# Another pitch for the hidden-state tiles of a two-layer decoder step: 272 and 288 words in place of 264

## The chip, the cores and the metric

One core of one Trainium2 chip runs the whole program in one launch. The metric is device time in microseconds (us), taken as the median of several runs. Engines are named as the profile names them: PE (TensorE matmul), PEld (TensorE weight load), DVE (VectorE), ACT (ScalarE), POOL (GpSimd) and SP (SyncE, which here only issues transfers).

## The reference

The program is one inference step of a two-layer decoder. It takes 264 tokens (256 of a prompt and 8 single-token samples), each a vector of 2048. Each layer is a mixer (retention, mLSTM and pooling heads behind one input projection and before one output projection) and a feed-forward block, which is the part that the change is about:

```python
def _layer(x, ...):
    ...                                        # mixers, x = x + rms_norm(mixed @ w_out)
    hn = _rms_norm(x, g_pre_ffn)
    ff = (jax.nn.silu(hn @ w_ffn_gate) * (hn @ w_ffn_up)) @ w_ffn_down
    x = x + _rms_norm(ff, g_post_ffn)
```

`w_ffn_gate` and `w_ffn_up` are 2048 x 5632, `w_ffn_down` is 5632 x 2048, all float32.

## The kernel before

**Products.** Activations lie transposed in the on-chip memory: 128 partitions hold 128 features, and a row of 264 words of 4 bytes holds the tokens. Each float32 product is made of three matmuls in a rounded float32 format (`F32R`): every weight and every activation is split into a high part and a low part, and high x high, high x low and low x high are added up in one PSUM bank. A matmul loads a weight tile of 128 x 128 (weight load, PEld) and streams an activation tile of 128 x 264 past it (PE). The function `chunk` (line 557) does this for a chunk of weights; its three parts follow each other, each over all tiles `k` of the chunk: `high` weights with the high tiles, `high` weights with the low tiles, `low` weights with the high tiles. Nearly all of these matmuls are recorded on line 572, and the few of a tile that is waited for last on lines 550 to 552.

**Stages of a layer.** The input projection and mixers run first, then the output projection (its activations are the tiles `mixed`), then the feed-forward block in two halves (`NBLK` = 2). Each half does gate and up projection for 22 hidden tiles (`BT` = 22; the activations are `ahi` and `alo`, 16 tiles each) and then the down projection (`down`, in PE's block): 16 output tiles, each from two chunks of 11 hidden tiles (`HT` = 11). So there are four down stages in the program. In a down stage the loop body is 8 chunks (four output tiles) and runs three times, with a last copy of it behind the loop.

**The hidden tiles.** For each hidden tile DVE multiplies the gate and up results, ACT copies the product into `hhi` (line 1245, which rounds it), and DVE subtracts to get the rest, `hlo` (line 1754). Line 634 hands both to the down projection as the streamed operand. `hhi` and `hlo` are laid over the region of `proj`, 48 tiles of 264 words, which the mixers have finished with by then.

**Where things lie.** `place` hands out regions of the on-chip memory one after the other, in bytes per partition: `x`, `ahi`, `alo` (16 x 264 words each), `raw` with `wlo` over it (4 x 2048 words), `whi` (2 x 2048 words), then `proj` with `mixed`, `hhi` and `hlo` over it. A tile `k` of `ahi`, `alo`, `hhi` or `hlo` starts `k` x 264 words behind the start of its array, so that consecutive tiles follow each other without a gap.

**Order of the work.** SP loads the weight chunks into four slots; ACT makes the high parts (line 941) and DVE the low parts (line 1306) two chunks ahead; DVE also empties the banks (lines 1711, 1741, 1745, 1771, 1773). All of it is tied together by counters written out by hand.

Of the kernel before, what the change touches and what calls it, by code (L numbers as in the profile page):

```python
# [18 lines left out]
F32R = mybir.dt.float32r  # L19
# [4 lines left out]
P = 128  # L24
D_MODEL, BATCH_S, SEQ, DEPTH, PAST = 2048, 8, 256, 2, 2048
TOK = SEQ + BATCH_S
# [8 lines left out]
BT = FT // NBLK  # L35
# [9 lines left out]
NPROJ = 48  # L45
# [97 lines left out]
FIRST_HI = [None, 0, 1, None]  # L143
AHEAD = [3, 4, 5, None]
SKEW = 4
UPDATES = [(0, 1), (1, 1)] + [(k, 2) for k in range(2, KT, 2)]
UPDATED_IN = [g for g, (_, n) in enumerate(UPDATES) for _ in range(n)]
N_UPD = len(UPDATES)
BANKS = 4
# [80 lines left out]
def build(nc, a, gamma, gchunk):  # L230
    with ExitStack() as ctx:
# [5 lines left out]
        def place(name, shape, dt, at=None):  # L237

            n = 4
            for s in shape[1:]:  # L240
                n *= s
            if at is None:
                at = used[0]
                used[0] += (n + 31) // 32 * 32
                assert used[0] <= 212800, (name, used[0])
            t = nc.alloc_sbuf_tensor_at(name, shape, dt, offset=start + at)
            return t, at
# [7 lines left out]
        x, _ = place("x", [P, KT, TOK], F32)  # L255
        ahi, _ = place("ahi", [P, KT, TOK], F32R)
        alo, _ = place("alo", [P, KT, TOK], F32R)
        raw, at_raw = place("raw", [P, RAW, CHUNK], F32)
        wlo, _ = place("wlo", [P, RAW, CHUNK], F32R, at_raw)
        whi, _ = place("whi", [P, HI, CHUNK], F32R)  # L260
        proj, at_proj = place("proj", [P, NPROJ, TOK], F32)
        mixed, _ = place("mixed", [P, NPROJ, TOK], F32R, at_proj)
        hhi, _ = place("hhi", [P, BT, TOK], F32R, at_proj)
        hlo, _ = place("hlo", [P, BT, TOK], F32R, at_proj + 4 * BT * TOK)
        table, _ = place("table", [P, sum(TABLE_SIZES)], F32)
        gains, _ = place("gains", [P, DEPTH, N_GAINS], F32)
        wpool, _ = place("wpool", [P, PG, P], F32)
        wgate, _ = place("wgate", [P, KT, 2 * MH], F32)
        gbias, _ = place("gbias", [P, DEPTH, 2], F32)
        sq, _ = place("sq", [P, 4, TOK], F32)  # L270
        ssq, _ = place("ssq", [P, TOK], F32)
        rms, _ = place("rms", [P, TOK], F32)
        rstd, _ = place("rstd", [P, TOK], F32)
        epsc, _ = place("epsc", [P, 1], F32)
        unread, _ = place("unread", [P, 1], F32)
        pick, _ = place("pick", [P, 4], F32)
        zero, _ = place("zero", [P, TOK], F32)
        ones_, _ = place("ones", [P, P], F32)
# [6 lines left out]
        def carve(region, at, *shapes):  # L285

            out = []
            for shape in shapes:
                n = 1
                for d in shape:  # L290
                    n *= d
                v = region[:, at:at + n]
                at += (n + 7) // 8 * 8
                if len(shape) == 2:
                    v = v.rearrange("p (a b) -> p a b", a=shape[0])
                if len(shape) == 3:
                    v = v.rearrange("p (a b c) -> p a b c", a=shape[0], b=shape[1])
                out.append(v)
            assert at <= region.shape[1] + 7, (at, region.shape)
            return out + [at]  # L300
# [7 lines left out]
        whi_spare, _ = place("whi_spare", [P, CHUNK], F32R, at_work + 4 * at_spare)  # L308
# [5 lines left out]
        selv, identv, maskv, rowsv, _ = carve(work, 0, (MH, P), (P,), (P,), (NR,))  # L314
# [9 lines left out]
        pa, pb, cut16, pwin, wsum, _ = carve(work, at_r, (PW,), (PW,), (16,), (PG, BATCH_S * 16), (PG, BATCH_S))  # L324
# [15 lines left out]
        gates, lfa, lfb, _ = carve(flat_sq, 0, (2, TOK), (TOK,), (TOK,))  # L340
# [3 lines left out]
        fourth_q, fourth_k, _ = carve(heads, 0, (KT, P), (KT, P))  # L344
        late = proj[:, T_MO:NPROJ, :].rearrange("p a t -> p (a t)")
        Cs, cdiag, _ = carve(late, 0, (BATCH_S, MV), (BATCH_S, MV))
# [155 lines left out]
        def _(pe):  # L502
            pe.wait_ge(*dve_done(3))
            for l in range(DEPTH):
# [75 lines left out]
                def first_three(c, o, m, e):  # L580

                    pe.wait_ge(*rms_made(l * 4 + e))
                    at_start = (l, m) == (0, 0)
                    skew = SKEW if at_start else 1
                    deferred = () if at_start else (2,) if m else (1, 2)
# [701 lines left out]
        def _(dve):  # L1287
# [6 lines left out]
            for l in range(DEPTH):  # L1294
# [27 lines left out]
                def scale_acc(m, k, n):  # L1322

                    u = 2 * l + m
                    dve.wait_ge(*acc_gained(u * KT + k + n))
                    dve.tensor_tensor(acc[:, k:k + n, :], acc[:, k:k + n, :],  # L1326
                                      rstd[:].rearrange("p (o t) -> p o t", o=1).broadcast_to([P, n, TOK]), ALU.mult)\
                        .then_inc(*scaled.up)

                def add_acc(g, k, n, done):  # L1330

                    dve.wait_ge(*scaled(g + 1))
                    dve.tensor_tensor(x[:, k:k + n, :], x[:, k:k + n, :], acc[:, k:k + n, :], ALU.add).then_inc(*done.up)  # L1333
# [11 lines left out]
                def into_operands(m, lay, m_next):  # L1345

                    c = lay * N_CHUNKS + (0, C_GU[0])[m_next]
                    base = (2 * l + m) * N_UPD
                    scale_acc(m, *UPDATES[0])
                    for g in range(N_UPD + 1):  # L1350
                        if g + 1 < N_UPD:
                            scale_acc(m, *UPDATES[g + 1])
                        if g < N_UPD:
                            add_acc(base + g, *UPDATES[g], x_updated)
                        if g >= 1:
                            k, n = UPDATES[g - 1]
                            for i in range(n):
# [695 lines left out]
```

## Time and profile before

| | us |
|---|---|
| median of 3 runs | 2467.01 |
| lowest and highest of them | 2466.32, 2468.39 |
| span of the profiled execution (first to last instruction) | 2466.6 |
| PE busy in that span | 2435.6 |

The time of the profiled execution itself is not listed apart from the three runs; its span is 0.4 us below their median. The page puts PE at 99% of the span and PE weight loads at 97%, DVE at 57%, ACT at 44%, POOL at 10%. A record of a matmul runs from its first streamed column to the end of its way through the array, so that the records of consecutive matmuls overlap: each lasts about 284 ns, and one starts every 121 ns.

### The profile page before, as it was taken

Reading aid. Unit: us, or ns where it says so; the run is one execution under the profiler, and the core shown is the slowest. Engines: PE = TensorE matmul, PEld = TensorE weight load, DVE = VectorE, ACT = ScalarE, POOL = GpSimd, SP = SyncE. Lnnn points to the kernel's source line nnn. Section 1 sums busy time; section 2 is a strip of 40 time slices with the busy share of each in tenths; the row PEclk is TensorE's granted clock in tenths of the full one; section 3 lists DMA queues with packets and bytes.
Section 4 is the critical chain, followed back from the end, with each engine's and each line's share of the span. In section 5 each row is a group of like instructions: output and inputs, shape, how many; then the busy total and the mean of one; then the engine's idle time right before and its main releaser. Section 6 shows DMA issues by size and latency. Waiting matters only on the chain.

```text
span 2466.6 us, 49136 instructions
## 1 busy us (share of the span) xinstructions
PE 2435.6 (99%) x20166; PEld 2387.1 (97%) x20166; DVE 1417.3 (57%) x1721; ACT 1088.0 (44%) x1419; POOL 246.2 (10%) x202
## 2 busy tenths in 40 slices
PE   9999999999999999999999999999999999999997
PEld 8999999899999999999999999998999999999997
DVE  5787564755544455554567866646555445555444
ACT  5444654543333343444444456545344333343443
POOL 1001334000000000002100014340000000000021
PEclk9999999999999999999999999999999999999999
DMA  8455545355545655545645555454555455555453
GB/s 301 164 172 197 196 164 187 137 180 177 187 159 185 202 174 184 183 159 184 222 151 169 173 200 197 167 175 139 185 182 177 167 183 195 187 175 182 163 185 130
DMA packets 71902, 443.87 MB, mean 180 GB/s; under 512 B 8656, under 2 KB 8880, under 8 KB 33136
## 3 DMA queue, kind: packets, MB, share of 16 engines
q1 hardware_dynamic: 64656, 415.40, 49.6%
q0 software_dynamic: 6992, 26.82, 3.5%
q8 instruction: 82, 1.34, 0.2%
q14 instruction: 28, 0.23, 0.0%
q10 hardware_dynamic: 144, 0.08, 0.0%
HBM read 427.10 MB, written 15.16 MB: 179 GB/s over the span
## 4 chain that ended last, share of the span: by engine, by line
PE 95%; DVE 3%; ACT 1%; issue 0%; DMA 0%; DVEq 0%; ACTq 0%
PE bank L572 86%; PE bank L550 1%; PE bank L551 1%; PE bank L552 1%; PE bank L651 1%; DVE work L1326 1%; PE bank L539 0%; DVE x L1333 0%; DVE wlo L1306 0%; PE bank L603 0%; PE bank L604 0%; PE bank L622 0%; PE bank L514 0%; DVE rstd L1319 0%; PE bank L816 0%
## 5 line engine op out<-in xcount | busy, mean ns | idle before, releaser
L1306 DVE TENSOR_TENSOR wlo<-raw,whi 128x2048 fp32r<-128x2048 f32 (+1 forms) x402 | 836.8, 2082 | 512.7 <-ACT whi L941 512.5
L941 ACT ACTIVATE whi<-raw 128x2048 fp32r<-128x2048 f32 (+1 forms) x406 | 709.4, 1747 | 883.8 <-PE bank L572 833.2
L572 PE MATMUL bank<-ahi,wlo 128*128 128x264 f32 x4096 | 537.9, 284 | 0.0
L572 PE MATMUL bank<-ahi,whi 128*128 128x264 f32 x4032 | 533.3, 285 | 0.0
L572 PE MATMUL bank<-alo,whi 128*128 128x264 f32 x4032 | 528.3, 284 | 0.0
L572 PEld LDWEIGHTS bank<-ahi,wlo 128*128 128x128 f32 x4096 | 512.2, 188 | 0.0
L572 PEld LDWEIGHTS bank<-ahi,whi 128*128 128x128 f32 x4032 | 505.0, 188 | 7.1 <-issue 3.1
L572 PEld LDWEIGHTS bank<-alo,whi 128*128 128x128 f32 x4032 | 503.9, 188 | 0.0
L572 PE MATMUL bank<-hhi,wlo 128*128 128x264 f32 x1392 | 190.1, 284 | 0.0
L572 PE MATMUL bank<-hlo,whi 128*128 128x264 f32 x1392 | 188.7, 283 | 0.0
L572 PE MATMUL bank<-hhi,whi 128*128 128x264 f32 x1392 | 188.6, 283 | 0.0
L572 PEld LDWEIGHTS bank<-hhi,wlo 128*128 128x128 f32 x1392 | 177.9, 188 | 0.1
L572 PEld LDWEIGHTS bank<-hhi,whi 128*128 128x128 f32 x1392 | 176.7, 188 | 0.0
L572 PEld LDWEIGHTS bank<-hlo,whi 128*128 128x128 f32 x1392 | 176.1, 188 | 0.0
L1818 POOL TENSOR_TENSOR ssq<-sq,ssq 128x264 f32<-128x264 f32 x56 | 118.5, 2117 | 264.2 <-ACT sq L963 264.2
L1245 ACT ACTIVATE hhi<-work 128x264 f32 (+1 forms) x88 | 37.4, 425 | 242.7 <-DVE work L1751 242.7
L1818 POOL TENSOR_TENSOR ssq<-sq,zero 128x264 f32<-128x264 f32 x4 | 8.6, 2160 | 1348.0 <-ACT sq L963 1329.9
L572 PE MATMUL bank<-mixed,whi 128*128 128x264 f32 x1016 | 128.4, 284 | 0.0
L572 PEld LDWEIGHTS bank<-mixed,whi 128*128 128x128 f32 x1016 | 125.4, 188 | 0.0
L1745 DVE TENSOR_TENSOR work<-bank,rstd 128x264 f32<-128x264 f32 x88 | 38.0, 432 | 135.1 <-PE bank L572 135.1
L1754 DVE TENSOR_TENSOR hlo<-work,hhi 128x264 f32 (+1 forms) x88 | 38.1, 433 | 60.1 <-ACT hhi L1245 60.1
L572 PE MATMUL bank<-mixed,wlo 128*128 128x264 f32 x508 | 68.0, 286 | 0.0
(311 smaller groups left out, 1817.2 us busy)
## 6 DMA issues: line engine op xcount, KB each, us to landing
raw<-w_gu SPq DMA_DIRECT2D x176, 1024.0 KB, 4.8
raw<-w_in SPq DMA_DIRECT2D x89, 1024.0 KB, 5.0
raw<-w_dn SPq DMA_DIRECT2D x128, 704.0 KB, 4.0
raw<-w_out SPq DMA_DIRECT2D x32, 1024.0 KB, 4.9
work<-s_ret POOLq DMA_DIRECT2D x12, 512.0 KB, 3.7
ret_s<-work POOLq DMA_DIRECT2D x12, 512.0 KB, 3.0
proj<-s_c POOLq DMA_DIRECT2D x8, 576.0 KB, 5.5
c_s<-proj POOLq DMA_DIRECT2D x8, 576.0 KB, 4.1
```

The lines of the kernel that those rows point to most:

```text
L550: pe.matmul(out, high[:, w], hi, start=first, stop=False)
L551: pe.matmul(out, high[:, w], lo, start=False, stop=False)
L552: return pe.matmul(out, low[:, w], hi, start=False, stop=last)
L572: mm = pe.matmul(out, weights[:, w], operand(tile)[of], start=start and part == 0 and k == 0, stop=stop and not late and part == 2 and k = ...
L651: return pe.matmul(out, in_, ident[0:n, 0:n], is_transpose=True, start=True, stop=True)
L941: act.activation(high[:, 0:words], raw[:, slot, 0:words], ACT.Copy).then_inc(*hi_made.up)
L1245: act.activation(hhi[:, i * 2 + u, :], hs[:, u, :], ACT.Copy).then_inc(*hidden_hi.up)
L1306: dve.tensor_tensor(wlo[:, slot, w], raw[:, slot, w], high[:, w].bitcast(F32), ALU.subtract)\
L1326: dve.tensor_tensor(acc[:, k:k + n, :], acc[:, k:k + n, :], rstd[:].rearrange("p (o t) -> p o t", o=1).broadcast_to([P, n, TOK]), ALU.mult)\
L1745: dve.tensor_tensor(ua[:, u, :], bank[j][:, 0:TOK], rstd[:], ALU.mult).then_inc(*tile_evac.up)
L1754: dve.tensor_tensor(hlo[:, i * 2 + u, :], hs[:, u, :], hhi[:, i * 2 + u, :].bitcast(F32), ALU.subtract).then_inc(*hidden_ready.up)
L1818: pool.tensor_tensor(ssq[:], sq[:, slot, :], zero[:] if first else ssq[:], ALU.add).then_inc(*sq_added.up)
```

## The change

The hidden tiles keep their size of 264 words, but the high tiles start every 272 words and the low tiles every 288 words, and the low array starts behind 22 x 272 words in place of 22 x 264. What lies between the tiles is left unused. Every instruction, its shape and its order stay as they are.

```diff
+PITCH_HI, PITCH_LO = 272, 288
...
-        hhi, _ = place("hhi", [P, BT, TOK], F32R, at_proj)
-        hlo, _ = place("hlo", [P, BT, TOK], F32R, at_proj + 4 * BT * TOK)
+        assert BT * (PITCH_HI + PITCH_LO) <= NPROJ * TOK
+        hhi = place("hhi", [P, BT, PITCH_HI], F32R, at_proj)[0][:, :, 0:TOK]
+        hlo = place("hlo", [P, BT, PITCH_LO], F32R, at_proj + 4 * BT * PITCH_HI)[0][:, :, 0:TOK]
```

## Rows read from the trace of the kernel before

**Rows 1.** The page, busy time, share of the span and count of each engine.

```profile
PE 2435.6 (99%) x20166; PEld 2387.1 (97%) x20166; DVE 1417.3 (57%) x1721; ACT 1088.0 (44%) x1419; POOL 246.2 (10%) x202
```

**Rows 2.** Windows: length, busy us (count) PE, PEld, DVE, ACT, POOL; PEclk, DMA share, GB/s.

```profile
451.00:714.00 263.00, 260.99 (x2147) 257.76 (x2148) 148.86 (x161) 109.98 (x127) 0.00 (x0) 0.99 0.49 168
714.00:841.50 127.50, 127.50 (x1059) 127.50 (x1058) 59.85 (x50) 45.19 (x33) 0.00 (x0) 1.00 0.56 187
...
2321.70:2449.30 127.60, 127.60 (x1057) 127.53 (x1056) 57.98 (x49) 55.42 (x64) 28.16 (x15) 1.00 0.49 164
...
455.00:456.30 1.30, 1.30 (x7) 1.11 (x6) 1.30 (x3) 0.80 (x4) 0.00 (x0) 0.50 0.00 0
```

**Rows 3.** Waits in the first down stage: total us, times, longest.

```profile
ACT whi L941 <- PE bank L572: 72.1, 27, 4.1
DVE wlo L1306 <- ACT whi L941: 52.0, 32, 2.9
```

**Rows 4.** The page's groups: one of three like it, and the writer of `hlo`.

```profile
L572 PE MATMUL bank<-hhi,wlo 128*128 128x264 f32 x1392 | 190.1, 284 | 0.0
...
L1754 DVE TENSOR_TENSOR hlo<-work,hhi 128x264 f32 (+1 forms) x88 | 38.1, 433 | 60.1 <-ACT hhi L1245 60.1
```

**Rows 5.** Timeline of PE, two like places in the first down stage: start, length.

```profile
753.48 0.28 PE L550 MATMUL bank<-hhi,whi 128*128 128x264 f32 x1
...
757.84 1.49 PE L572 MATMUL bank<-hhi,whi 128*128 128x264 f32 x11
...
817.23 0.28 PE L550 MATMUL bank<-hhi,whi 128*128 128x264 f32 x1
```

**Rows 6.** Timeline of PE in gate/up: parts of one chunk.

```profile
603.79 2.10 PE L572 MATMUL bank<-ahi,whi 128*128 128x264 f32 x16
605.73 2.10 PE L572 MATMUL bank<-alo,whi 128*128 128x264 f32 x16
```

**Rows 7.** Timeline of PE at 455 us, first and last of five.

```profile
455.11 0.42 PE L550 MATMUL bank<-ahi,whi 128*128 128x264 f32 x1
...
455.99 0.42 PE L604 MATMUL bank<-alo,whi 128*128 128x264 f32 x1
```

**Rows 8.** The tile `ahi`, eight instants: the two matmuls running, ns min/median/max.

```profile
L572 PE MATMUL bank<-ahi,whi x2: 282/284/285, 603.8 to 603.9; 128*128 128x264 f32 x2
L572 PE MATMUL bank<-ahi,whi x2: 282/283/284, 603.9 to 604.0; 128*128 128x264 f32 x2
L572 PE MATMUL bank<-ahi,whi x2: 282/283/284, 604.0 to 604.2; 128*128 128x264 f32 x2
L572 PE MATMUL bank<-ahi,whi x2: 278/280/282, 604.2 to 604.3; 128*128 128x264 f32 x2
L572 PE MATMUL bank<-ahi,whi x2: 278/280/283, 604.3 to 604.4; 128*128 128x264 f32 x2
L572 PE MATMUL bank<-ahi,whi x2: 283/286/288, 604.4 to 604.5; 128*128 128x264 f32 x2
L572 PE MATMUL bank<-ahi,whi x2: 288/288/288, 604.5 to 604.6; 128*128 128x264 f32 x2
L572 PE MATMUL bank<-ahi,whi x2: 285/286/288, 604.6 to 604.8; 128*128 128x264 f32 x2
```

**Rows 9.** The tiles `hhi` and `hlo`, instants at 758.0, 758.4 and 759.5 us.

```profile
L572 PE MATMUL bank<-hhi,whi x2: 278/280/282, 757.8 to 758.0; 128*128 128x264 f32 x2
...
L572 PE MATMUL bank<-hhi,whi x2: 288/288/288, 758.2 to 758.3; 128*128 128x264 f32 x2
...
L572 PE MATMUL bank<-hlo,whi x2: 279/280/282, 759.3 to 759.4; 128*128 128x264 f32 x2
```

**Rows 10.** Timeline of PE in the output projection: one chunk and the next start.

```profile
374.45 4.04 PE L572 MATMUL bank<-mixed,whi 128*128 128x264 f32 x32
378.33 2.12 PE L572 MATMUL bank<-mixed,wlo 128*128 128x264 f32 x16
380.29 0.90 PE L572 MATMUL bank<-mixed,whi 128*128 128x264 f32 x6
```

## The prediction

> **What bounds the kernel now.** I read the page first, for the engine that is busy: PE, with 2435.6 of 2466.6 us [rows 1]. Then windows over single stages, since a share over the whole program is a mean. In a down stage, the only stage whose reads the change moves, PE is busy for the whole window, 127.50 of 127.50 us, while DVE works 59.85 and ACT 45.19 [rows 2]; gate and up projection is as full, 260.99 of 263.00, the rest being its start. The waits of the first down stage run one way: ACT waits 72.1 us for PE to free a weight slot, DVE 52.0 us for ACT [rows 3], and PE is not in the list. So the reader is to see that here time is a count of matmuls times the distance from one start to the next, and nothing else; what the other engines do has some 65 us of room in each down stage.
>
> The count: four down stages, 32 chunks each, 33 matmuls a chunk, 4224, of which 1408 each are high weights on `hhi`, high weights on `hlo`, low weights on `hhi` (1392 of each stand on line 572 [rows 4], the other 16 on lines 550 to 552). The distance: the same matmul of the loop body comes at 753.48 and, two bodies of 264 matmuls on, at 817.23 us [rows 5], so 63.75/528 = 120.74 ns. 4224 of these are 510.0 us, the sum of the four windows. In gate and up projection 16 matmuls take 605.73 - 603.79 = 1.94 us, about 121 ns [rows 6].
>
> Is 120.7 ns a floor? No row shows one there. At 455 us the granted clock is 0.50, the 1.2 GHz level [rows 2], and five matmuls of the same size start 0.88/4 = 0.22 us apart [rows 7], which is just 264 columns at 1.2 GHz. In the down stages the clock is 1.00 [rows 2], the 2.4 GHz level; half of 220 ns is 110, and 10.7 ns are on top. So at the upper level something other than the array's clock slows the stream, and the question is whether the place of the streamed tile has a part in it.
>
> The Trainium skill (TensorE: Matmul & The Clock Gate, Back-to-back issue gap) gives N/2.4 + 2.5 ns for a matmul alone at the upper clock, 112.5 ns here; the trace disagrees, with 120.7. If the change brought the down stages to that figure, 8.2 ns x 4224 = 35 us would go, an estimate from that page.
>
> **Does the place matter? What the rows show.** A matmul's recorded length contains its time on the stream. At eight instants in a row of one gate/up chunk two matmuls are running, tiles 0 and 1, then 1 and 2, and so on [rows 8]. Pair by pair this solves to lengths of tiles 0 to 7: 285, 282, 284, 282, 278, 283, 288, 288 ns, and tile 8 is 285 again. The tiles are 1056 bytes apart, 4 x 256 + 32, so tile k starts at 32k modulo 256 bytes, and after eight tiles the place comes round. Is it the place, or the position in the chunk? In the down projection the 11 tiles from 757.84 us [rows 5] are tiles 11 to 21 of `hhi`: line 550 closes the second chunk of the body, the third takes 4 us, and this is the fourth, which like every second chunk takes the upper 11 tiles. `ahi` starts 16896 = 66 x 256 bytes into the arena, and `proj`, where `hhi` starts, at 99840 = 390 x 256, so both count from the same place. The first two, 11 and 12, last 278 and 282, the fourth and fifth, 14 and 15, both 288 [rows 9]: what tiles 4 and 3, 6 and 7 of `ahi` have. So the place goes with the length, over a range of 10 ns. But the law is not clean: `hlo` starts 22 x 1056 bytes further on, which is 192 modulo 256, so its tiles 12 and 13, the second and third of that chunk, stand where tiles 2 and 3 of `ahi` do, and last 279 and 282 in one order or the other, not 284 and 282 [rows 9]. What came before also counts, and a new order of places can settle on a new pattern.
>
> **The change, part by part.**
>
> *The places.* The high pitch is 1088 bytes, 4 x 256 + 64: the tiles start at 0, 64, 128, 192 modulo 256, with 6, 6, 5 and 5 of 22 tiles. Lengths by place: 6 x 285 + 6 x 284 + 5 x 278 + 5 x 288 = 6244, mean 283.8 ns. The low array starts 22 x 1088 = 23936 bytes on, 128 modulo 256, and its pitch of 1152 is 4 x 256 + 128, so low tiles start at 128 and 0 in turn: (278 + 285)/2 = 281.5 ns. Two in three matmuls stream `hhi`, one in three `hlo`: 283.05 ns. Before, all eight places: 2270/8 = 283.75. The difference is 0.70 ns a matmul, and 0.70 x 4224 = 3.0 us gained.
>
> Bounds of this term, from the same rows: every matmul at the best place, 278 against 283.75, -5.75 x 4224 = -24 us; every one at the worst, 288, +18 us. Between them I take the sum by places, because the two arrays go through four and two places and a mean over places has held elsewhere: 120.7 and 121 ns in two stages with different arrays.
>
> The Trainium skill (SBUF — State Buffer, Specifications (TRN2)) gives lines of 16 bytes and says that a read pays for each new line of 16 bytes that it crosses into. A tile is 66 such lines at all three pitches, so by that rule the term is 0 and the time stays. The lengths of 278 to 288 ns for equal tiles show that it is not the whole of it.
>
> *The gaps.* Consecutive tiles no longer touch (32 bytes of gap in `hhi`, 96 in `hlo`). The nearest rows are the output projection, whose tiles are taken out of order and partly apart: a chunk of 48 takes 380.29 - 374.45 = 5.84 us, 121.7 ns each, and its last 16, the low weights, 1.96 us, 122.5 ns [rows 10]. Against 120.74 that is +0.9 to +1.8 ns, on 4224 matmuls +4.0 to +7.5 us. That chunk differs in places as well as in gaps, so I count nothing of it in the sum and keep it as a rival.
>
> *The writers.* ACT and DVE write the 88 high and 88 low tiles at new places; the low ones take 433 ns each [rows 4]. If the place changed that by as much as a matmul's, 10 in 284, it would be 15 ns each, under 3 us for both kinds together, in a stretch where DVE idles 60.1 us just before these very instructions [rows 4]. Counted at nothing. If that cover were gone, only the last tile of each of four halves is waited for directly: 4 x 2 x 15 ns, 0.1 us.
>
> *What else might be late.* Nothing is added to a queue, no transfer or wait moves. If the down stages ran as fast as 110 ns a matmul, they would last 116 us, against 60 us of DVE and a DMA share of 0.56 [rows 2], so no other engine becomes the bound.
>
> *Sum.* 2466.6 us of span and the 0.4 us by which the median lies above it, less 3.0: 2464.0 us.
>
> **The rivals.**
>
> 1. *A worse order.* The new order of places and gaps settles like that of the output projection. Place: the down stages; price +0.9 to +1.8 ns a matmul, up to 2467.0 + 7.5; I name +1.4 ns, 2473. It decides for slower from +1.17 ns on (4.9 us). For it: those rows, and that the down stages are now at the lowest distance of the three stages shown. Against: the low tiles avoid the two places with 288 ns altogether.
>
> 2. *A good lock.* With only two places in turn for `hlo` and four for `hhi`, the stream settles at the quick end and stays there. The low tiles of [rows 9] ran at 279 and 282, mean 280.5, 3.25 ns below 283.75. Over all matmuls this is -13.7 us; over two thirds of them -9.2 us. I name 2456. For it: lengths depend on what came before, so a short cycle of places need not give the mean. Against: nothing picks the quick end over the slow one.
>
> 3. *The 10.7 ns go.* If they come from an awkward start of the tiles, and starts at multiples of 64 bytes cure it, 10.7 x 4224 = 45 us: 2422. Against it: before, every second tile already starts at a multiple of 64 relative to the array, and those four lengths (285, 284, 278, 288, mean 283.75) are no better than the other four (282, 282, 283, 288, also 283.75).
>
> 4. *The place is not the cause*, and the lengths follow a rhythm of PE itself that only looks like it: 2467.
>
> **How the numbers follow.** One measurement of this kernel can tell about 0.2%, 4.9 us, from no change. The sum by places 0.42, its own range 2460 to 2468 (1 ns a matmul either way, as far as the stages differ); a worse order 0.18; a good lock 0.30; the full gain 0.03; no effect 0.07. Faster by over 0.2%: 0.26 of the lock, 0.03, and 0.09 of the first case, 0.38. Slower: 0.16 of the worse order and 0.01 of the rest, 0.17. Within: 0.45. The range runs from the lock's full price of 13.7 us, 2453, to the worse order at 2474, and leaves out the far end of the lock, the full gain and +1.8 ns a matmul.
>
> **What would show it.** In the profile after: the distance of the same matmul over loop bodies (120.74 before) should be near 120.0; lengths of matmuls on `hlo` should take two values near 278 and 285, those on `hhi` four; gate and up projection must stay at 121. 119.5 or less shows the lock, 121.9 or more the worse order, 112 or so the full gain. The prediction is wrong if lengths do not follow places in the new order, so that the sum by places has no ground, or if a stage that the change does not touch moves.

## The result and the profile after

| us | before | after |
|---|---|---|
| median of 9 runs each | 2467.31 | 2472.49 |
| lowest and highest | 2466.27, 2468.39 | 2471.92, 2475.11 |
| span of the profiled execution | 2466.6 | 2473.3 |

The ratio is 1.0024, 95% interval 1.0014 to 1.0033. The change makes the kernel 5.2 us slower where 3.0 us less were forecast.

First the page after: its busy times, and the three groups of down-stage matmuls (count, busy us, mean ns of one record).

```profile
PE 2443.1 (99%) x20166; PEld 2395.0 (97%) x20166; DVE 1418.1 (57%) x1721; ACT 1088.3 (44%) x1419; POOL 247.9 (10%) x202
...
L576 PE MATMUL bank<-hhi,wlo 128*128 128x264 f32 x1392 | 192.7, 286 | 0.0
L576 PE MATMUL bank<-hlo,whi 128*128 128x264 f32 x1392 | 190.4, 284 | 0.0
L576 PE MATMUL bank<-hhi,whi 128*128 128x264 f32 x1392 | 189.1, 283 | 0.0
```

The last two of these groups before the change, beside the one of [rows 4]:

```profile
L572 PE MATMUL bank<-hlo,whi 128*128 128x264 f32 x1392 | 188.7, 283 | 0.0
L572 PE MATMUL bank<-hhi,whi 128*128 128x264 f32 x1392 | 188.6, 283 | 0.0
```

PE and its weight loads have grown, by 7.5 and 7.9 us; DVE and ACT stand within 1 us of where they stood [rows 1]. Of the three groups, low weights with `hhi` gained most, 190.1 to 192.7 us [rows 4], although only the places of activations were moved. Next the windows over the first down stage and the gate/up half behind it (columns as in [rows 2]).

```profile
715.40:844.20 128.80, 128.80 (x1058) 128.80 (x1057) 59.92 (x50) 45.17 (x33) 0.00 (x0) 1.00 0.56 186
844.20:1099.40 255.20, 255.20 (x2114) 255.20 (x2113) 135.87 (x131) 100.49 (x97) 0.00 (x0) 1.00 0.53 178
```

The stage took 127.50 us and now takes 128.80, with PE busy throughout and the granted clock at 1.00, the 2.4 GHz level, as before [rows 2]. So no wait has come in, and it is not the clock. The waits of that stage:

```profile
ACT whi L945 <- PE bank L576: 73.2, 27, 4.1
DVE wlo L1310 <- ACT whi L945: 52.4, 32, 2.9
```

They run the same way as in [rows 3] and have grown with the stage, by 1.1 and 0.4 us. Then PE's timeline: two parts in gate/up, the three parts of one chunk with the start of the next, and two like places two loop bodies apart (start, length).

```profile
605.23 2.10 PE L576 MATMUL bank<-ahi,whi 128*128 128x264 f32 x16
607.16 2.10 PE L576 MATMUL bank<-alo,whi 128*128 128x264 f32 x16
...
755.30 0.28 PE L554 MATMUL bank<-hhi,whi 128*128 128x264 f32 x1
...
755.67 1.49 PE L576 MATMUL bank<-hhi,whi 128*128 128x264 f32 x11
756.99 1.50 PE L576 MATMUL bank<-hlo,whi 128*128 128x264 f32 x11
758.33 1.52 PE L576 MATMUL bank<-hhi,wlo 128*128 128x264 f32 x11
759.69 0.53 PE L576 MATMUL bank<-hhi,whi 128*128 128x264 f32 x3
...
819.69 0.28 PE L554 MATMUL bank<-hhi,whi 128*128 128x264 f32 x1
```

The same matmul comes 64.39 us later, 64.39/528 = 121.95 ns a matmul, where [rows 5] give 120.74. In gate/up it is 1.93/16, about 121 ns, as in [rows 6]. The difference, 1.21 ns x 4224 = 5.1 us, is the whole of the medians' 5.2. The three parts of the chunk do not share it alike: 1.32, 1.34 and 1.36 us for 11 matmuls, 120.0, 121.8 and 123.6 ns.

Of the 6.7 us between the two profiled spans, 1.4 lie ahead of the first down stage, which starts at 715.4 in place of 714.0. Most of that is the clock's and not the change's. Windows over the first matmuls of gate/up, before and then after:

```profile
454.00:461.00 7.00, 6.40 (x42) 5.33 (x43) 7.00 (x15) 4.82 (x14) 0.00 (x0) 0.76 0.00 0
454.00:461.00 7.00, 6.36 (x32) 5.08 (x31) 7.00 (x14) 4.98 (x14) 0.00 (x0) 0.51 0.00 0
```

In these 7 us the mean granted clock was 0.76 in the execution before and 0.51 in the one after, which stood longer at the 1.2 GHz level (0.50). In other profiles it was 1.00 there (e6, e8) or 0.54 (e5), whatever the arrangement, so this is one part of the scatter of single times.

Last the tiles themselves: all matmuls on `hlo`, two pairs of neighbours among them, and the writers of both arrays, that of `hhi` after and before (ns minimum, median, maximum).

```profile
L576 PE MATMUL bank<-hlo,whi x1392: 281/283/289, 716.8 to 2454.5; 128*128 128x264 f32 x199
L576 PE MATMUL bank<-hlo,whi x2: 288/288/289, 761.1 to 761.3; 128*128 128x264 f32 x2
L576 PE MATMUL bank<-hlo,whi x2: 283/284/286, 761.5 to 761.6; 128*128 128x264 f32 x2
L1758 DVE TENSOR_TENSOR hlo<-work,hhi x88: 432/434/436, 484.2 to 2331.3; 128x264 f32 x76, 128x264 fp32r<-128x264 f32 x12
...
L1249 ACT ACTIVATE hhi<-work x88: 423/424/426, 483.7 to 2330.8; 128x264 f32 x76, 128x264 fp32r<-128x264 f32 x12
L1245 ACT ACTIVATE hhi<-work x88: 423/424/427, 482.3 to 2325.4; 128x264 f32 x76, 128x264 fp32r<-128x264 f32 x12
```

The low tiles start at two places only, 128 and 0 modulo 256 bytes, for which 278 and 285 ns were forecast. None lasts 278; two neighbours, one at either place, last 288 and 289, and a moment later a pair lasts 283 and 286. The writers have not changed: 424 ns for `hhi` as before, 434 for `hlo` after 433 [rows 4].

### The profile page after: what moved, and what is told of

The parts are those of the page before. It is cut to its first block, busy times and chain, and to the rows that moved or that the text cites. A ratio compares the mean times of both kernels' runs of the same rounds, so it can differ in the third digit from the quotient of the medians.

```text
span 2473.3 us, 49165 instructions
## 1 busy us (share of the span) xinstructions
PE 2443.1 (99%) x20166; PEld 2395.0 (97%) x20166; DVE 1418.1 (57%) x1721; ACT 1088.3 (44%) x1419; POOL 247.9 (10%) x202
## 3 DMA queue, kind: packets, MB, share of 16 engines
q8 instruction: 82, 1.34, 0.2%
## 4 chain that ended last, share of the span: by engine, by line
PE 95%; DVE 3%; ACT 1%; issue 0%; DMA 0%; DVEq 0%; ACTq 0%
PE bank L576 86%; PE bank L554 1%; PE bank L555 1%; PE bank L556 1%; PE bank L655 1%; DVE work L1330 0%; PE bank L543 0%; DVE wlo L1310 0%; DVE x L1337 0%; PE bank L607 0%; PE bank L608 0%; PE bank L626 0%; PE bank L518 0%; DVE rstd L1323 0%; PE bank L820 0%
## 5 line engine op out<-in xcount | busy, mean ns | idle before, releaser
L576 PE MATMUL bank<-hhi,wlo 128*128 128x264 f32 x1392 | 192.7, 286 | 0.0
```

The source lines that it names most:

```text
L576: mm = pe.matmul(out, weights[:, w], operand(tile)[of], start=start and part == 0 and k == 0, stop=stop and not late and part == 2 and k = ...
```

## Experiments

Below, "distance" is the time from the first to the last matmul of the first down stage, by their number less one; "parts" are its means over the chunks of the second and third loop body (without the chunk of lines 550 to 552), for high weights on `hhi`, high weights on `hlo`, low weights on `hhi`. Places are starts of the arrays, bytes modulo 256, `hhi` and `hlo`. A distance goes by the starts of matmuls alone, since the profile models their ends. It repeats within 0.01 ns where nothing in the down stages differs (e12 and e15, one kernel twice; before and e16, 120.73 both), far better than a device time does; 1 ns of it is 4.2 us.

| kernel | pitch in words; places | distance, ns | parts, ns | time, us | ratio [95%] |
|---|---|---|---|---|---|
| before | 264, 264; 0, 192 | 120.73 | 120.5, 120.6, 121.2 | 2467.5 | |
| after | 272, 288; 0, 128 | 121.96 | 120.8, 121.9, 123.3 | 2472.5 | 1.0024 [1.0014, 1.0033] |
| e1 | 272, 264; 0, 128 | 121.62 | 121.5, 120.7, 122.7 | 2471.0 | 1.0015 [1.0005, 1.0025] |
| e2 | 264, 288; 0, 128 | 121.84 | 121.6, 121.9, 122.0 | 2472.8 | 1.0023 [1.0013, 1.0032] |
| e3 | 264, 264; 128, 64 | 121.29 | 120.8, 122.4, 120.7 | 2470.1 | 1.0011 [1.0001, 1.0021] |
| e4 | 576, 576; 0, 128 | 121.42 | 121.0, 121.6, 121.5 | 2470.5 | 1.0013 [1.0003, 1.0022] |
| e5 | 264, 264, low read backwards; 0, 96 | 121.99 | 121.6, 121.8, 122.5 | 2474.7 | one run |
| e6 | 264, 312; 0, 96 | 121.99 | 121.6, 121.8, 122.5 | 2472.5 | one run |
| e7 | 272, 288; 128, 0 | 121.82 | 122.0, 122.1, 121.7 | 2472.7 | one run |
| e8 | 264, 264; 0, 96 | 120.98 | 120.6, 120.7, 121.4 | 2467.5 | one run |
| e9 | 264, 264; 0, 192, weights +128 | 121.29 | 120.8, 122.4, 120.7 | 2471.9 | one run |
| e10 | 576, 576; 0, 32 | 120.73 | 120.1, 121.1, 120.6 | 2467.5 | 1.0000 [0.9990, 1.0009] |
| e11 | 576, 576; 128, 160 | 120.78 | 120.0, 121.9, 119.9 | 2468.4 | one run |
| e12, e15 | 576, 576; 0, 224 | 120.29 | 119.8, 120.7, 120.1 | 2466.5 | 0.9996 [0.9987, 1.0005] |
| e17 | 272, 288; 0, 192 | 120.91 | 121.5, 119.9, 121.2 | 2469.2 | one run |
| e18 | 272, 288; 0, 160 | 121.69 | 121.0, 122.5, 121.2 | 2472.3 | one run |

The kernel before, run beside them, had medians of 2467.5 us (e1 to e4, e9 to e12) and 2467.3 (e13 to e16), and in one run each 2469.2 (e5 to e8) and 2468.2 (e17, e18). Where there was one run, the distance decides.

### Which part of the change costs? (e1 to e4)

**e1**, the high pitch alone, and **e2**, the low pitch alone, take the place of the two lines that lay out the tiles; so do the pairs of lines in the later diffs.

```diff
-        hhi, _ = place("hhi", [P, BT, TOK], F32R, at_proj)
-        hlo, _ = place("hlo", [P, BT, TOK], F32R, at_proj + 4 * BT * TOK)
# e1
+        hhi = place("hhi", [P, BT, 272], F32R, at_proj + 0)[0][:, :, 0:TOK]
+        hlo = place("hlo", [P, BT, 264], F32R, at_proj + 23936)[0][:, :, 0:TOK]
# e2
+        hhi = place("hhi", [P, BT, 264], F32R, at_proj + 0)[0][:, :, 0:TOK]
+        hlo = place("hlo", [P, BT, 288], F32R, at_proj + 23424)[0][:, :, 0:TOK]
```

> High tiles every 272 words, low tiles still every 264 (low array starts 128 bytes modulo 256 from the arena's base in place of 192). Mean distance of two matmuls in a down stage: 120.73 ns before, 121.96 after the change; by parts of a chunk (high weights on hhi, high on hlo, low on hhi) 120.5, 120.6, 121.2 before and 120.8, 121.9, 123.3 after. Theory A, the order of start places (modulo 256 bytes) sets the distance, with history over some tiles: the cost came mostly with the low tiles' two places, so about 121.0 here, parts 120.8, 120.6, 121.5, and about 2468.5 us. Theory B, every gap between consecutive tiles costs: two matmuls in three have a gap, 121.5 ns, parts 1 and 3 slow, part 2 not, about 2470.5 us. Theory C, the weights and the tile together (low weights on hhi are slow because of the pitch of hhi): parts 1 and 3 as after, 120.8 and 123.3, mean 121.5.

> Low tiles every 288 words at the same two places as after the change (128 and 0 modulo 256), high tiles still every 264. Theory A (order of places with history): part 2 as after, 121.9, part 3 partly, 122, part 1 as before, mean about 121.5, 2470.5 us. Theory B (gaps cost): only part 2 has gaps, 121.9, parts 1 and 3 as before, mean 121.1, 2468.8 us. Theory C (weights and tile together): part 3 as before, 121.2, mean 121.1.

Each costs most of the loss by itself, +0.89 and +1.11 ns, and both together +1.23, so the costs don't add. By itself e1 looks like Theory B, gaps: parts 1 and 3 are slow and part 2 is not. e2 speaks against it: the first part on `hhi`, whose tiles had neither moved nor got gaps, went from 120.5 to 121.6, and the mean to 121.84 where Theory B had 121.1. No part has a price of its own.

**e3**, the old pitches with both arrays 128 bytes further on, and **e4**, every tile at one of two places.

```diff
# e3
+        hhi = place("hhi", [P, BT, 264], F32R, at_proj + 128)[0][:, :, 0:TOK]
+        hlo = place("hlo", [P, BT, 264], F32R, at_proj + 23360)[0][:, :, 0:TOK]
# e4
+        pairs = place("pairs", [P, BT, 576], F32R, at_proj + 0)[0]
+        hhi, hlo = pairs[:, :, 0:TOK], pairs[:, :, 288:288 + TOK]
```

> Pitch 264 for both as before, but both arrays start 128 bytes further on. Theory A: lengths follow the place, so every length moves by four tiles along hhi (the shortest, 278 ns, stood at tile 12, now at tiles 8 and 16), while the mean distance stays, 120.7 ns and 2467 us. Theory D, a rhythm of PE that has nothing to do with the place: lengths stay at the tiles where they were, mean 120.7. Theory B expects no change of the mean either.

> High and low tiles in turn in one array with a pitch of 576 words, 2304 bytes = 9 x 256: every high tile starts at place 0 modulo 256, every low tile at place 128. Theory A: no variety of places, so the stream settles on one short pattern; its mean can lie anywhere in the range of lengths seen, 278 to 288 ns against a mean of 283.75, so a distance between 115 and 125 ns, clearly off 120.7 or 122.0, with few lengths. Theory B (gaps cost): every matmul has a gap, 122.5 ns or more, 2474 us or more. Theory D (place has no part): 120.7 ns, 2467 us, and eight lengths as before.

e3 was expected to leave the mean where it was, since its tiles go through all eight places as before; it came to 121.29. With all of `hhi` at place 0, e4 stands at 121.42, and its lengths are no one number: in long stretches they run through 288, 285, 278, 283, 283 and again, at one and the same place. In others they stand still. The first part of one and the same chunk of the loop body, without its first matmul, in the first body and in the second:

```profile
L572 PE MATMUL bank<-pairs,whi x10: 281/281/281, 732.7 to 733.8; 128*128 128x264 f32 x10
L572 PE MATMUL bank<-pairs,whi x10: 278/283/288, 764.7 to 765.8; 128*128 128x264 f32 x10
```

These are the same instructions, with the same tiles, weight slots and bank. They stand 120.0 ns apart in the first body and 121.7 in the second, in all four down stages alike, so what was streamed before them decides.

### Gaps, or places? (e5 to e8)

**e5** reads the low tiles backwards from an array without gaps; **e6** has the same places in the same order, 96 - 32k, with gaps of 192 bytes.

```diff
# e5
-                    return hhi[:, k, :], hlo[:, k, :]
+                    return hhi[:, k, :], hlo[:, BT - 1 - k, :]
...
-                                dve.tensor_tensor(hlo[:, i * 2 + u, :], hs[:, u, :], ...
+                                dve.tensor_tensor(hlo[:, i * (-2) + (BT - 1 - u), :], hs[:, u, :], ...
# e6
+        hhi = place("hhi", [P, BT, 264], F32R, at_proj + 0)[0][:, :, 0:TOK]
+        hlo = place("hlo", [P, BT, 312], F32R, at_proj + 23392)[0][:, :, 0:TOK]
```

> Pitch 264 for both, but the low tiles are stored in reverse, tile 0 last: they touch each other, and start places go back by 32 bytes modulo 256 from tile to tile, from place 96. This run stands beside e6_gap_back, which has the same start places modulo 256 with gaps. Theory A, only the sequence of start places modulo 256 and what went before count: both runs have the same lengths, matmul by matmul, and one mean distance, somewhere between 120.3 and 122.3 ns. Theory B, gaps cost: no gap here, so 120.7 ns here and over 121.1 in the other.

> High tiles every 264 words, low tiles every 312 words (1248 bytes, 224 modulo 256, so places go back by 32), low array starting so that tile k has the same place modulo 256 as in e5_low_reversed, with gaps of 192 bytes. Theory A: the same lengths and the same mean as there, within 0.1 ns. Theory B: part 2 of the chunks (high weights on hlo) slower by 1 ns or more than there.

The tile `hlo` of e5 and two like places of its timeline:

```profile
L572 PE MATMUL bank<-hlo,whi x1392: 281/284/288, 716.4 to 2454.1; 128*128 128x264 f32 x199
...
754.97 0.28 PE L550 MATMUL bank<-hhi,whi 128*128 128x264 f32 x1
...
819.38 0.28 PE L550 MATMUL bank<-hhi,whi 128*128 128x264 f32 x1
```

The same of e6:

```profile
L572 PE MATMUL bank<-hlo,whi x1392: 281/284/288, 714.3 to 2451.8; 128*128 128x264 f32 x199
...
752.83 0.28 PE L550 MATMUL bank<-hhi,whi 128*128 128x264 f32 x1
...
817.24 0.28 PE L550 MATMUL bank<-hhi,whi 128*128 128x264 f32 x1
```

Both take 64.41 us for two bodies, and matmul by matmul all 4224 lengths agree within 1 ns. Pitch and gap do not count; the places in their order do. And the order counts much: e5 reads the very places of before (all eight, in an array without gaps), and is 1.26 ns slower.

**e7** shifts the changed kernel's arrays by 128 bytes; **e8** keeps the pitches of before with the low array at e6's first place.

```diff
# e7
+        hhi = place("hhi", [P, BT, 272], F32R, at_proj + 128)[0][:, :, 0:TOK]
+        hlo = place("hlo", [P, BT, 288], F32R, at_proj + 24064)[0][:, :, 0:TOK]
# e8
+        hhi = place("hhi", [P, BT, 264], F32R, at_proj + 0)[0][:, :, 0:TOK]
+        hlo = place("hlo", [P, BT, 264], F32R, at_proj + 23392)[0][:, :, 0:TOK]
```

> The change's own pitches, 272 and 288, both arrays 128 bytes further on. If the loss belongs to the two pitches (or to their gaps), the mean distance stays at 122.0 ns. If it belongs to the sequence of places at which each part begins and the history that it carries over (Theory A as it stands after e3_shift128), the mean moves by 0.3 ns or more either way, in 120.5 to 122.5.

> Pitch 264 for both, the low array starting at place 96 modulo 256 in place of 192, so that from the last high tile of a part to the first low tile the place goes on by 32 as it does within a part. If each change of array upsets the settled pattern because the step of places breaks, one of three breaks goes: part 2 settled throughout, 120.3 to 120.8 ns, mean 120.5 or less, about 2466 us. If steps at the change of array have nothing to do with it, the mean lies anywhere in 120.3 to 121.8 and part 2 is no better than the 120.55 of before.

e7 turns the parts round (122.0 on the first, 121.7 on the last), but its mean, 121.82, moved by 0.14 ns only, less than the 0.3 expected if the start decides: by itself it speaks for the pitches. In e8 the part behind the mended step did not settle (120.7), so a break of the step at the change of array is not the price. e8 at 120.98, against e6's 121.99, has the same first low place and steps of +32 instead of -32.

### Place against what? (e9)

**e9** leaves the pitches and moves the weight arrays: a pad of 32 words ahead of `raw` (which `wlo` lies over) and one ahead of `proj`, so that every weight is 128 bytes further on against the tiles, which keep their places modulo 256.

```diff
+        place("pad0", [P, 32], F32)
...
+        place("pad1", [P, 32], F32)
         proj, at_proj = place("proj", [P, NPROJ, TOK], F32)
```

> Pitch 264 as before; only the weight arrays (raw with wlo over it, whi) lie 128 bytes further on against all tiles. Theory A with the tile's own address: nothing moves, lengths of ahi tiles 0 to 7 stay 285, 282, 284, 282, 278, 283, 288, 288 ns and the down stages stay at 120.73 ns. Theory C, the place of the tile against that of the weights counts: the pattern moves by four tiles along ahi (278 at tile 0 in place of tile 4), and the down stages go to the 121.29 ns of e3_shift128.

The tile `ahi` of e9, the first two instants of a gate/up chunk, tiles 0 and 1, then 1 and 2:

```profile
L574 PE MATMUL bank<-ahi,whi x2: 278/280/283, 603.8 to 603.9; 128*128 128x264 f32 x2
L574 PE MATMUL bank<-ahi,whi x2: 283/286/288, 603.9 to 604.0; 128*128 128x264 f32 x2
```

In [rows 8] tiles 0, 1 and 2 last 285, 282 and 284 ns. Here they last 278, 283 and 288, which there are tiles 4, 5 and 6, those 128 bytes further round. No activation was touched. In the down stages 4210 of 4224 lengths agree within 1 ns with e3, which moved the tiles and not the weights, and the starts say the same: part by part the distances are e3's. So a matmul's length goes by where its tile starts against where the weights lie.

One rival is left: the pads also move what the transfers, ACT and DVE write, so it could be their traffic that slows PE, and no run moves that alone. Against it stands the kernel before: in its fourth down stage POOL works 28.16 us and ACT 55.42, in the first 0.00 and 45.19 [rows 2], and still 1052 of its 1056 lengths are those of the first within 1 ns.

The Trainium skill (TensorE: Matmul & The Clock Gate, Step-by-step: what each phase is for) has two independent read ports, for the streamed operand and for weight loads, and says that loading the next weights takes no read bandwidth from the running matmul. The lengths of e9 disagree in so far as the place of the weights shows in the stream; e14, below, is on the side of the page as to the volume.

### A lock on one place? (e10 to e12, e15)

The high and low tiles lie in pairs, 576 words apart, so that every high tile starts at one place and every low tile at another.

```diff
+        pairs = place("pairs", [P, BT, 576], F32R, at_proj + 0)[0]
# e10
+        hhi, hlo = pairs[:, :, 0:TOK], pairs[:, :, 264:264 + TOK]
# e11: as e10, with at_proj + 128
# e12 and e15
+        hhi, hlo = pairs[:, :, 0:TOK], pairs[:, :, 312:312 + TOK]
```

> High and low tiles in turn, pitch 576 words (9 x 256 bytes), low tile right behind its high tile: high tiles all at place 0, low tiles all at place 32. In e4_one_place (0 and 128) stretches settled at 120.0 ns a matmul, others on a cycle of five with 121.3. Theory A: where the place stays the same, 120.0 is the best pattern seen; with only 32 bytes between the two places the upset at each change of array should be small, mean 120.0 to 120.6, 2464 to 2467 us, the best arrangement so far. Against it: if every change of array costs whatever the step, 121 or more.

> As e10_pairs_32, everything 128 bytes further on: high tiles at 128, low tiles at 160. With the same place throughout, a settled pattern can't know which place it is, unless some places are worse in themselves: if the mean and the lengths are those of e10_pairs_32 within 0.2 ns, only the order counts; if not, the place itself has a part.

> As e10_pairs_32 with the low tile 312 words behind its high tile: high tiles at place 0, low tiles at 224. Theory A: near e10_pairs_32, 120.0 to 121.0 ns, with other lengths at the changes of array.

> The same kernel as e12_pairs_back32 (high and low tiles in turn, pitch 576, low tile 312 words behind its high tile), timed: 120.29 and 120.48 ns in place of 120.73 and 120.93, 0.44 x 4224 = 1.9 us, so 2465.5 us and a ratio of 0.9992, at the edge of what the rounds tell from 1.

The tile `pairs` of e10 in a stretch of ten matmuls:

```profile
L572 PE MATMUL bank<-pairs,whi x10: 281/281/281, 751.4 to 752.5; 128*128 128x264 f32 x10
```

Ten in a row last 281 ns and stand exactly 120.0 ns apart. Elsewhere in the same kernel the same tiles run through e4's cycle of five at about 121.3 ns, so here too what ran before decides. The mean of the stage, 120.73, is that of the kernel before and not the 120.0 to 120.6 expected. In e11 the settled length is 284 instead of 281, at the same 120.0 ns:

```profile
L572 PE MATMUL bank<-pairs,wlo x3: 284/284/284, 753.5 to 753.8; 128*128 128x264 f32 x3
```

So a record's length is not the distance. The means of e10 and e11 agree within 0.05 ns, their lengths do not: by the expectation of e11 the place itself has a part too. Two like places of e12's timeline:

```profile
753.69 0.28 PE L550 MATMUL bank<-pairs,whi 128*128 128x264 f32 x1
...
817.19 0.28 PE L550 MATMUL bank<-pairs,whi 128*128 128x264 f32 x1
```

63.50/528 = 120.27 ns is the quickest down stage of all runs. It would be worth 0.44 x 4224 = 1.9 us; e15, the same kernel timed, has 0.9996 [0.9987, 1.0005], no difference that can be measured. None of the versions beats the kernel before measurably.

### The volume of weights, the low weights, the order (e13, e14, e16)

**e13** is the changed kernel with the second part of each down-stage chunk left out; **e14** is the kernel before with half of the weight columns in the down stages.

```diff
# e13
+                        if part == 1 and operand is of_hidden:
+                            continue
# e14
+                    wide = P // 2 if operand is of_hidden else P
...
-                            w = bass.ds((tile - min(ks)) * P, P)
-                            mm = pe.matmul(out, weights[:, w], operand(tile)[of], ...
+                            w = bass.ds((tile - min(ks)) * P, wide)
+                            mm = pe.matmul(out[0:wide], weights[:, w], operand(tile)[of], ...
```

> The changed kernel (272 and 288) without the second part of each chunk of the down stages: the low tiles are not streamed there, save the last tile of a half, so high times low is left out of the down product. Each chunk is high weights on hhi, then low weights on hhi, with no change of array between. If history from the change of array made the third part slow (123.3 ns), it now runs at 121.0 or less, as the first part (120.8). If the low weights themselves make it slow with this pitch, it stays at 122.5 or more.

> The kernel before, with the weights of the down stages cut to 64 of 128 columns: half of the output features are not computed there. If the stream of the tile is slowed by the load of the next weights, which reads half as many bytes here, the distance of two matmuls falls from 120.7 to about 115 ns, half of the 10.7 ns above 110. If the load has no part in it, the distance stays at 120 to 121.5.

e13 (2307.96 us, one run) asked why low weights on `hhi` cost 123.3 ns in the changed kernel and high weights 120.8, on the same tiles. Neither answer held: with no part between them both run at 121.8. Not only the third part was slow through its surroundings, the first was quick through them. For e14 (2468.86 us, one run), the weight loads of the tile `hhi`, before and then in e14, and two like places of e14's timeline:

```profile
L572 PEld LDWEIGHTS bank<-hhi,whi x1392: 187/188/189, 713.9 to 2446.3; 128*128 128x128 f32 x199
L573 PEld LDWEIGHTS bank<-hhi,whi x1392: 133/134/138, 715.4 to 2446.8; 128*64 128x64 f32 x199
...
754.96 0.28 PE L550 MATMUL bank<-hhi,whi 128*64 128x264 f32 x1
...
818.71 0.28 PE L550 MATMUL bank<-hhi,whi 128*64 128x264 f32 x1
```

A load takes 134 ns in place of 188, and the distance stays: 63.75/528 = 120.74. The 10.7 ns above 110 are not paid by volume of weights; my expectation of 115 fell. (The parts did shift, to 121.1, 120.5 and 120.5.)

**e16** moves nothing in memory. Gate and up and input projection take their 16 tiles in the order 0, 8, 1, 9, ..., so that tiles at like places follow each other.

```diff
-                    chunk(c, slot, hi_slot, bank[j][:, 0:TOK], operand, range(KT), True, True, norm=norm,
+                    chunk(c, slot, hi_slot, bank[j][:, 0:TOK], operand,
+                          [k + 8 * g for k in range(KT // 2) for g in range(2)] if operand is of_x else range(KT), True, True, norm=norm,
```

> The kernel before with another order of the 16 tiles in the chunks of the input projection and of gate and up projection: 0, 8, 1, 9 and so on, so that two tiles of the same place modulo 256 follow each other. Nothing moves in memory. If repeated places settle near 120.0 ns, as in the arrays of pairs, these chunks fall from 120.83 to 120.0 to 120.5 ns and some 11,700 matmuls save 4 to 10 us, 2457 to 2463 us. If a step of 0 and 32 in turn settles as badly as the steps of 64 and 128 did, 121.5 ns or more, 2475 us.

The timeline of e16 in gate/up, and last two like places of the kernel before, four chunks apart:

```profile
606.05 2.12 PE L572 MATMUL bank<-ahi,whi 128*128 128x264 f32 x16
608.01 2.12 PE L572 MATMUL bank<-alo,whi 128*128 128x264 f32 x16
...
611.92 2.12 PE L572 MATMUL bank<-ahi,whi 128*128 128x264 f32 x16
...
599.93 2.10 PE L572 MATMUL bank<-alo,whi 128*128 128x264 f32 x16
...
623.13 2.10 PE L572 MATMUL bank<-alo,whi 128*128 128x264 f32 x16
```

5.87/48 = 122.3 ns, against 23.20/192 = 120.8 before, while the down stages, untouched, stay at 120.73. The kernel takes 2483.23 us, ratio 1.0067 [1.0052, 1.0082]. That is slower than the worse of the two outcomes expected, 2475. Same tiles, same places, same weights, another order (each weight tile goes along with its activation tile, whereas e5 turned the activation tiles alone): 16 us. A price for each place cannot give that, since the sum over places is unchanged.

### Is it the pitches? (e17, e18)

The changed kernel's pitches with only the low array further on, by 64 bytes (e17) and by 32 (e18).

```diff
+        hhi = place("hhi", [P, BT, 272], F32R, at_proj + 0)[0][:, :, 0:TOK]
# e17
+        hlo = place("hlo", [P, BT, 288], F32R, at_proj + 24000)[0][:, :, 0:TOK]
# e18
+        hlo = place("hlo", [P, BT, 288], F32R, at_proj + 23968)[0][:, :, 0:TOK]
```

> The change's pitches, 272 and 288, the low array 64 bytes further on: low tiles at places 192 and 64 in place of 128 and 0. If steps of 64 and 128 bytes from tile to tile are bad in themselves, the mean distance stays at 121.7 to 122.3 ns. If the start of the low array is what made it bad, the mean moves to 121.2 or less, or to 122.5 or more, as three starts with a pitch of 264 lay at 120.73, 120.98 and 121.29.

> As e17_after_low64, the low array 32 bytes further on than in the change: low tiles at places 160 and 32, which no high tile has. Steps bad in themselves: 121.7 to 122.3 ns again. Start of the low array decides: outside of that.

PE's timeline of e17 and, last, its tile `hlo`:

```profile
753.97 0.28 PE L550 MATMUL bank<-hhi,whi 128*128 128x264 f32 x1
...
755.66 1.49 PE L572 MATMUL bank<-hlo,whi 128*128 128x264 f32 x11
756.99 0.28 PE L572 MATMUL bank<-hhi,wlo 128*128 128x264 f32 x1
...
817.80 0.28 PE L550 MATMUL bank<-hhi,whi 128*128 128x264 f32 x1
...
L572 PE MATMUL bank<-hlo,whi x1392: 278/280/289, 715.8 to 2448.6; 128*128 128x264 f32 x199
```

63.83/528 = 120.89 ns: with the pitches of the change, 64 bytes on the low array take back 1.05 of the 1.23 ns. The median on `hlo` is 280 ns, after 283. e18, at 121.69, came out as expected of steps that are bad in themselves, and so did e7. So with the pitches of the change three starts lie at 121.7 to 122.0 ns and one at 120.9, while with a pitch of 264 the three starts lay at 120.73, 120.98 and 121.29. The pitches alone do not fix the cost: it comes from the order of places that they give together with the start. Whether such pitches are worse than 264 on the whole, these few starts do not show.

## Why the prediction was wrong, point by point

**What bounds the kernel: right.** Matmuls times distance; the whole difference is distance, 1.21 ns on 4224.

**"Does the place matter?": right, and short of one thing.** Places do go with lengths, but against the weights' place (e9), and only in a given order (e16, and e4 and e10, where one place has lengths from 278 to 288 or a steady 281, by what ran before).

**"The places" is the step that failed.** It took the lengths that eight places have in steps of +32 bytes, carried them over to steps of 64 and 128, and chose the sum by places "because the two arrays go through four and two places and a mean over places has held elsewhere". The two stages which showed that mean both go in steps of +32: they were one case, not two. In its place the runs showed that the distance belongs to the order as a whole: +1.23 ns where -0.70 stood, on `hlo` lengths from 281 to 289 where 278 and 285 stood. The prediction had the warning in its own words, that `hlo` at the places of tiles 2 and 3 did not have their lengths [rows 9], and the sum went past it. It also took a difference of lengths for one of distances, which it need not be: over the first down stage the lengths of e11 are on average 0.9 ns above those of the kernel before, and its distance 0.05.

**"The gaps": right to count them at nothing**, e5 and e6 being alike within 1 ns matmul by matmul. But the rows behind that paragraph, the output projection in another order of tiles [rows 10], were the only ones in which the tiles do not come in steps of +32 throughout: by `MIX_HI` and `MIX_LO` of the kernel its high tiles come in three runs, and six of its low tiles in steps of 96. They priced another order at +0.9 to +1.8 ns; +1.2 came.

**The writers, what else might be late: right.** 424 and 434 ns for a tile, no new wait, gate/up at 121 ns.

**The rivals.** The first, a worse order, is what happened: 2473 named, 2472.49 measured, its mechanism shown by e5, e16 and e17. That the size came so near is in part luck: other orders lay anywhere from -0.44 ns (e12) to +1.26 (e5). What stood against it, that the low tiles avoid the two places with 288 ns, was the same wrong step again: they lasted 288 and 289 at two others. A good lock exists, as e10's stretches at 120.0, but the best whole stage gained 0.44 ns and not 3.25. The 10.7 ns did not go in any arrangement. That the place is not the cause is excluded by e17 against the changed kernel, which differ in 64 bytes of one start.

**What stays open.** What makes the 10 ns above 110 was not found: it is not the volume of weights (e14), nor gaps (e5, e6). How tile and weights act on each other, and so what distance a new order will have, cannot be worked out from these runs; only that it goes by the order, and lay, as the mean of the first down stage (in e13 without PE's waits) or of gate/up, between 120.3 and 122.3 ns in every one. The Trainium skill (SBUF — State Buffer, Specifications (TRN2)) has reads pay for each new line of 16 bytes; a tile is 66 such lines in all of these runs, so the spread of 2 ns is not told by that rule.

## What to carry to other kernels

Where the engine that sets the time streams without a gap, moving its operands is not free, and lengths per address taken from one order of reading don't sum to the time of another: look for a stage that already reads in the new kind of order, and price by that. Two stages that agree are evidence only if they differ in what the change alters. When a layout loses a little, try other starts of the same layout, and measure the distance of like matmuls over loop bodies, which here told 0.1 ns, 0.4 us, where single times of one kernel lay 3 us apart.

## What was not expected of the hardware

- Weight arrays 128 bytes further on shift the lengths of matmuls on untouched tiles: 278 ns instead of 285 for the first (e9).
- The order alone of 16 tiles is worth 1.46 ns a matmul, 16 us in the kernel (e16).
- The same instructions of a loop body, with nothing moved, stand 120.0 ns apart in one pass and 121.7 in the next, by what was streamed before (e4).
- With one place throughout, the stream settles at exactly 120.0 ns, or runs a cycle of five at about 121.3 (e10, e4).
- Half of the weight columns shorten the weight load from 188 to 134 ns and leave the distance at 120.74 ns (e14).
- A matmul's recorded length can differ at one distance: 281 and 284 ns, both 120.0 ns apart (e10, e11).
